# Delta-rule inverse on one orientation, with a PE turn of two heads at once and products between all four quarters of the array

## The reference

```python
a_mat = where(strict, einsum('bhnid,bhnjd->bhnij', k * beta, k) * decay, 0.0) + eye(64)
rhs = concatenate([v * beta, k * beta * exp(g)], axis=-1)
sol = triangular_solve(a_mat, rhs, left_side=True, lower=True)      # one per chunk, head and direction
u, w = sol[..., :128], sol[..., 128:]
def step(s, xs):                                                    # a scan over the chunks
    v_new = u_c - w_c @ s
    o = qd_c @ s + qk_c @ v_new
    s = s * ge_c + ke_c.T @ v_new
```

## Time and profile before

| | us |
|---|---|
| median of 3 runs | 2147.72 (2143.14 to 2150.04) |
| the profiled execution, its own time | 2146.08 |
| its span in the trace | 2144.3 |
| the stretch of the inversion, first level to the start of L2061 | 1076.9 to 1235.1 |
| PE busy over the span | 92% |
| DVE busy | 55% |
| ACT busy | 47% |

### The profile page before, as it was taken

How to read it: one execution, slowest core, us unless ns; L and a number is a source line. 1 busy time by engine, 2 the same in 40 slices (tenths; PEclk the granted TensorE clock), 3 DMA queues, 4 the chain that set the end, 5 groups by cost and what they waited for, 6 DMA issues and landing times.

```text
span 2144.3 us, 41573 instructions
## 1 busy us (share of the span) xinstructions
PE 1962.7 (92%) x16842; PEld 1729.2 (81%) x16842; DVE 1186.6 (55%) x1809; ACT 1016.2 (47%) x1592; POOL 157.3 (7%) x151
## 2 busy tenths in 40 slices
PE   6998899888899999989888889999979999898997
PEld 5783588786787787868778879999969998678997
DVE  4421578643543243354356657656767656677754
ACT  5332367523441143244633246544756655366653
POOL 0000100001000000100134410000011001011000
PEclk8999899868999999989999999999999999899999
DMA  8340268531233332333200046665545664415653
GB/s 262 97 123 29 70 206 248 160 104 42 76 98 88 89 98 88 91 90 87 70 4 4 4 117 170 186 178 149 160 116 148 185 174 146 123 45 152 186 173 113
DMA packets 441804, 254.60 MB, mean 119 GB/s; under 512 B 10817, under 2 KB 440513, under 8 KB 441537
## 3 DMA queue, kind: packets, MB, share of 16 engines
q1 hardware_dynamic: 441664, 252.59, 40.5%
HBM read 251.51 MB, written 1.05 MB: 118 GB/s over the span
## 4 chain that ended last, share of the span: by engine, by line
PE 84%; DVE 9%; ACT 3%; issue 2%; DMA 1%; POOL 0%; DVEq 0%; ACTq 0%; SPq 0%; POOLq 0%
PE bank L380 21%; PE bank L382 20%; PE bank L381 20%; PE bank L372 4%; PE bank L594 2%; PE bank L595 2%; PE bank L1958 2%; DVE weights_lo L330 2%; ACT weights_hi L323 1%; PE bank L932 1%; PE bank L1159 1%; PE bank L602 1%; PE bank L1975 1%; PE bank L1972 1%; DVE h L2578 1%
## 5 line engine op out<-in xcount | busy, mean ns | idle before, releaser
L330 DVE TENSOR_TENSOR weights_lo<-ring,weights_hi 128x1024 fp32r<-128x1024 f32 x472 | 578.0, 1228 | 363.6 <-ACT weights_hi L323 359.4
L380 PE MATMUL bank<-x_hi,weights_hi 128*128 128x256 f32 (+1 forms) x2024 | 647.2, 320 | 68.7 <-DVE x_lo L527 19.3
L323 ACT ACTIVATE weights_hi<-ring 128x1024 fp32r<-128x1024 f32 x472 | 495.4, 1054 | 389.1 <-PE bank L382 367.7
L382 PE MATMUL bank<-x_hi,weights_lo 128*128 128x256 f32 (+1 forms) x2024 | 637.7, 315 | 0.0
L381 PE MATMUL bank<-x_lo,weights_hi 128*128 128x256 f32 (+1 forms) x2024 | 637.3, 315 | 0.0
L380 PEld LDWEIGHTS bank<-x_hi,weights_hi 128*128 128x128 f32 x2024 | 389.6, 192 | 104.8 <-issue 71.0
L381 PEld LDWEIGHTS bank<-x_lo,weights_hi 128*128 128x128 f32 x2024 | 389.5, 192 | 25.8 <-issue 1.4
L382 PEld LDWEIGHTS bank<-x_hi,weights_lo 128*128 128x128 f32 x2024 | 389.0, 192 | 23.3
L380 PE MATMUL bank<-hidden_hi,weights_hi 128*128 128x256 f32 (+1 forms) x864 | 272.5, 315 | 10.0 <-DVE hidden_lo L1502 6.8
L382 PE MATMUL bank<-hidden_hi,weights_lo 128*128 128x256 f32 (+1 forms) x864 | 272.3, 315 | 0.0
L381 PE MATMUL bank<-hidden_lo,weights_hi 128*128 128x256 f32 (+1 forms) x864 | 271.6, 314 | 0.0
(11 more groups left out here) (370 smaller groups left out, 2391.4 us busy)
## 6 DMA issues: line engine op xcount, KB each, us to landing
ring<-mlp_w SPq DMA_DIRECT2D x128, 512.0 KB, 4.0
ring<-ada_w SPq DMA_DIRECT2D x96, 512.0 KB, 4.6
ring<-w_ffn_in SPq DMA_DIRECT2D x88, 512.0 KB, 4.0
ring<-w_ffn_out SPq DMA_DIRECT2D x32, 512.0 KB, 3.9
ring<-gdn_w_in SPq DMA_DIRECT2D x24, 512.0 KB, 3.9
ring<-even_w_in SPq DMA_DIRECT2D x18, 512.0 KB, 4.7
ring<-w_out SPq DMA_DIRECT2D x16, 512.0 KB, 4.0
ring<-w_in_a SPq DMA_DIRECT2D x14, 512.0 KB, 3.8
```

The source lines that it names most:

```text
L323: nc.scalar.activation(w_hi[:, g % AHEAD, :], ring[:, g % RAW, :], ACT.Copy).then_inc(hi_done[g % AHEAD].sem, 1)
L330: nc.vector.tensor_tensor(w_lo[:, g % AHEAD, :], ring[:, g % RAW, :], w_hi[:, g % AHEAD, :].bitcast(F32), ALU.subtract).then_inc(lo_done[g ...
L380: pe.matmul(dst, lhs[0](k), rhs[0](k), start=start and k == 0, stop=False)
L382: last = pe.matmul(dst, lhs[1](k), rhs[0](k), start=False, stop=stop and k == nk - 1)
```

## The change

`XX`, the second orientation, is gone. In each level PE makes the 16 products NA.XT of a unit so that even heads land on one half and odd heads on the other, and chunk 0 in one bank and chunk 1 in the other (L1963 of the changed kernel): they go between all four quarters. Then 8 transposes, each of two heads of one chunk (64 rows, 128 columns) onto all partitions (L1968), put the turned `XT` into the second half of the same two banks. ACT copies both banks to the new tile `QX` (L2152). PE makes 16 products between all quarters (L1978) and DVE copies under the mask in two halves, even and odd heads, of 128x4x64 each (L2230). `first` loses the two products that made the other orientation (L1945), ACT one copy of the unit matrix for each unit (L2134), DVE the copies of L2218 and L2226. The scaled inverses go to `XB` (a part of `QX`) and to `XW`, which all passes share.

```diff
-        DE0, NA0, XT0, XX0, QQ, GL, BB, kends = (co(2, NH, C) for _ in range(8))
+        DE0, NA0, XT0, _, QX, _, GL, BB, kends = (co(2, NH, C) for _ in range(9))
+        QX = arena[:, gdn_at + 4 * UNIT:gdn_at + 6 * UNIT].rearrange("p (z c m n) -> p z c m n", z=2, c=2, m=2)
...
         def pe_gdn_first(pe, p):
-                for c in range(2):
-                    pe.matmul(bank_of(p, z, 1)[half(1 - c), :], eye64[half(c), :], na[half(c), z].rearrange("p h c -> p (h c)"),
-                              start=True, stop=True)
...
         def pe_gdn_q(pe, p, lv):
+            xt = XT[p % 2]
             for z, u in units(p):
                 pe.wait_ge(N["xt"], nth(LEVELS + 1, p, lv, z))
-                for hd in range(NH):
+                for hp in range(4):
                     for c in range(2):
-                        ins = pe.matmul(bank_of(p, z, 0)[half(1 - c), hd * C:(hd + 1) * C], NA[p % 2][half(c), z, hd, :],
-                                        XT[p % 2][half(c), z, hd, :], start=True, stop=True)
-                ins.then_inc(N["q"], 1)
+                        for par in range(2):
+                            hd = 2 * hp + par
+                            pe.matmul(bank_of(p, z, c)[half(par), hp * C:(hp + 1) * C], NA[p % 2][half(c), z, hd, :],
+                                      xt[half(c), z, hd, :], start=True, stop=True)
+                for hp in range(4):
+                    for c in range(2):
+                        two = xt[half(c), z, 2 * hp:2 * hp + 2, :].rearrange("p h c -> p (h c)")
+                        ins = pe.transpose(bank_of(p, z, c)[:, (4 + hp) * C:(5 + hp) * C], two, eye64[half(c), :])
+                ins.then_inc(N["xr"], 1)
 
         def pe_gdn_z(pe, p, lv):
             for z, u in units(p):
-                pe.wait_ge(N["qc"], nth(LEVELS, p, lv, z))
-                pe.wait_ge(N["xx"], nth(LEVELS, p, lv, z))
-                xx = XX[p % 2]
-                for hd in range(NH):
-                    col = slice(hd * C, (hd + 1) * C)
-                    if lv < LEVELS - 1:
-                        for c in range(2):
-                            r = half(1 - c)
-                            pe.matmul(bank_of(p, z, 1)[r, col], QQ[r, z, hd, :], xx[r, z, hd, :], start=True, stop=True)
+                pe.wait_ge(N["qx"], nth(LEVELS, p, lv, z))
+                for hp in range(4):
+                    col = slice(hp * C, (hp + 1) * C)
                     for c in range(2):
-                        r = half(1 - c)
-                        ins = pe.matmul(bank_of(p, z, 0)[half(c), col], xx[r, z, hd, :], QQ[r, z, hd, :], start=True, stop=True)
+                        for par in range(2):
+                            ins = pe.matmul(bank_of(p, z, par)[half(c), col], QX[half(par), z, c, 1, col], QX[half(par), z, c, 0, col],
+                                            start=True, stop=True)
                 ins.then_inc(N["zz"], 1)
...
         def act_gdn_level(act, p, lv):
             for z, u in units(p):
-                act.wait_ge(N["q"], nth(LEVELS, p, lv, z))
-                nc.scalar.activation(QQ[:, z], compact(bank_of(p, z, 0)), ACT.Copy).then_inc(N["qc"], 1)
+                act.wait_ge(N["xr"], nth(LEVELS, p, lv, z))
+                for c in range(2):
+                    ins = nc.scalar.activation(QX[:, z, c].rearrange("p m n -> p (m n)"), bank_of(p, z, c)[:, :], ACT.Copy)
+                ins.then_inc(N["qx"], 1)
...
         def dve_gdn_level(dve, p, lv):
                 dve.wait_ge(N["zz"], nth(LEVELS, p, lv, z))
-                nc.vector.copy_predicated(xt[:, z], mask(levels[:, z, lv, :]), compact(bank_of(p, z, 0))).then_inc(N["xt"], 1)
-                if lv < LEVELS - 1:
-                    nc.vector.copy_predicated(xx[:, z], mask(levels[:, 1 - z, lv, :]), compact(bank_of(p, z, 1)))\
-                        .then_inc(N["xx"], 1)
+                m = levels[:, z, lv, :].rearrange("p (o c) -> p o c", o=1).broadcast_to((P, NH // 2, C)).bitcast(I32)
+                for par in range(2):
+                    ins = nc.vector.copy_predicated(xt[:, z].rearrange("p (h r) c -> p h r c", r=2)[:, :, par, :], m,
+                                                    four(bank_of(p, z, par)))
+                ins.then_inc(N["xt"], 1)
```

More of the change, by code:

```diff
@@ L1555, in two_block_kernel @@
         gdn_at = co.at
-        DE0, NA0, XT0, XX0, QQ, GL, BB, kends = (co(2, NH, C) for _ in range(8))
+        DE0, NA0, XT0, _, QX, _, GL, BB, kends = (co(2, NH, C) for _ in range(9))
+        QX = arena[:, gdn_at + 4 * UNIT:gdn_at + 6 * UNIT].rearrange("p (z c m n) -> p z c m n", z=2, c=2, m=2)
         def by_heads(x, c):
             return x.rearrange("p (z h c) -> p z h c", z=2, c=c)
-        DE1, NA1, XT1, XX1 = (by_heads(spare[:, i * UNIT:(i + 1) * UNIT], C) for i in range(4))
-        DE, NA, XT, XX = (DE0, DE1), (NA0, NA1), (XT0, XT1), (XX0, XX1)
+        DE1, NA1, XT1, XW = (by_heads(spare[:, i * UNIT:(i + 1) * UNIT], C) for i in range(4))
+        DE, NA, XT = (DE0, DE1), (NA0, NA1), (XT0, XT1)
+        XB = QX[:, :, 0].rearrange("p z m (h i) -> p z (m h) i", i=C)
         last_state = by_heads(arena[:, gdn_at:gdn_at + UNIT], P)
@@ L1566, in two_block_kernel @@
         last_QKT = by_heads(arena[:, gdn_at + 2 * UNIT:gdn_at + 4 * UNIT], P)
-        last_U = by_heads(arena[:, gdn_at + 5 * UNIT:gdn_at + 7 * UNIT], P)
+        last_U = by_heads(arena[:, gdn_at + 6 * UNIT:gdn_at + 8 * UNIT], P)
         qdc, SG = co(2, NH // 2, P), co(2, NH // 2, NDV)
@@ L1864, in dve_odd_in @@
             normed(VB - 1)
-        gdn_names = ("gl", "g", "d", "size", "e", "bb", "eb", "kk", "aa", "eye", "first", "q", "qc", "zz", "xt", "xx", "xb", "xw",
+        gdn_names = ("gl", "g", "d", "size", "e", "bb", "eb", "kk", "aa", "eye", "first", "xr", "qx", "zz", "xt", "xb", "xw",
                      "u", "uc", "wt", "wtc", "kend", "ws", "vn", "su", "ss", "sg", "clear", "qk", "eu", "qkt", "g2", "qe", "qd",
@@ L1943, in pe_gdn_first @@
                 na = NA[p % 2]
-                for c in range(2):
-                    pe.matmul(bank_of(p, z, 1)[half(1 - c), :], eye64[half(c), :], na[half(c), z].rearrange("p h c -> p (h c)"),
-                              start=True, stop=True)
                 for hd in range(NH):
                     for c in range(2):
-                        ins = pe.matmul(bank_of(p, z, 0)[half(c), hd * C:(hd + 1) * C], na[half(c), z, hd, :], eye64[half(c), :],
-                                        start=True, stop=True)
+                        ins = pe.matmul(bank_of(p, z, 0)[half(c), hd * C:(hd + 1) * C], na[half(c), z, hd, :], eye64[half(c), :], start=True, stop=True)
@@ L1983, in pe_gdn_values @@
                     for c in range(2):
-                        ins = pe.matmul(b[half(c), (hd % 4) * P:(hd % 4 + 1) * P], QQ[half(c), z, hd, :],
+                        ins = pe.matmul(b[half(c), (hd % 4) * P:(hd % 4 + 1) * P], XB[half(c), z, hd, :],
                                         vtok[half(c), TBS[p][z], hd * P:(hd + 1) * P], start=True, stop=True)
@@ L1994, in pe_gdn_weights @@
                         ins = pe.matmul(four(bank_of(p, z, c))[half(hd % 2), hd // 2, :],
-                                        ktk[half(c), TBS[p][z], hd * C:(hd + 1) * C], XX[p % 2][half(c), z, hd, :],
+                                        ktk[half(c), TBS[p][z], hd * C:(hd + 1) * C], XW[half(c), z, hd, :],
                                         start=True, stop=True)
@@ L2132, in act_gdn_eyes @@
                     act.wait_ge(N["xw"], u - 4 + 1)
-                nc.scalar.activation(XT[p % 2][:, z], heads(eye64), ACT.Copy)
-                nc.scalar.activation(XX[p % 2][:, z], heads(eye64), ACT.Copy).then_inc(N["eye"], 1)
+                nc.scalar.activation(XT[p % 2][:, z], heads(eye64), ACT.Copy).then_inc(N["eye"], 1)
         def act_gdn_decay(act, p):
@@ L2217, in dve_gdn_first @@
                     .then_inc(N["xt"], 1)
[L2218 removed]
         def dve_gdn_level(dve, p, lv):
[L2221 removed]
+            xt = XT[p % 2]
             for z, u in units(p):
                 dve.wait_ge(N["zz"], nth(LEVELS, p, lv, z))
[L2224 to L2228 removed]
+                m = levels[:, z, lv, :].rearrange("p (o c) -> p o c", o=1).broadcast_to((P, NH // 2, C)).bitcast(I32)
[3 more added lines that the diff above has]
+                ins.then_inc(N["xt"], 1)
+                if lv == LEVELS - 1:
                     dve.wait_ge(N["xt"], nth(LEVELS + 1, p, LEVELS, z))
[L2230 removed]
+                    nc.vector.tensor_tensor(XB[:, z], xt[:, z], per_head(beta[:, TBS[p][z], z * NH:(z + 1) * NH]), ALU.mult)\
                         .then_inc(N["xb"], 1)
```

8 lines of the change are left out of this document (2 added, 6 removed).

## The result

| | before | changed |
|---|---|---|
| median, same chip | 2146.99 us (2143.14 to 2152.77, 6 runs) | 2127.34 us (2122.25 to 2130.29, 6 runs) |
| ratio | | 0.9915 [0.9897, 0.9932] |
| span of the profiled execution | 2144.3 | 2125.5 |

The change is faster by 19.65 us, 0.9% of the time.

What follows compares the result with a forecast made beforehand. PE was taken as the bound, partly held by instructions arriving. 15.8 us less PE work, 9.0 us of new waits and 9 us fewer code stalls made -15.8, so 2132 us, range 2122 to 2142.

Steps and rivals of the forecast that it cites:

- array work: PE's first products, turns and second products in 20 levels, with `first`: 15.8 us less PE work together.
- New waits: PE waiting for ACT's two copies in seven levels, 6.3 us, and DVE's subtractions in six, 2.7: 9.0 us more.
- Code: PE's stalls for arriving instructions, 14.1 us: with 1472 fewer instructions a third is left, 9 us less.
- The counts: PE's instructions and trace: 1472 fewer instructions, some 33 packets on the instruction queue, "issue" from 14 us to about 5.
- First products and turn: Each level on PE: both units' first products 1.95 us to 1.0, with 1.12 us added for turning both.
- Rival A: The turn on PE is dear because transposes go singly: 9 us more, 2140 us; chance 0.15.
- D (two quarters): First products of even and odd heads don't overlap in four quarters: 20 us more, 2152 us; chance 0.06.
- `first`: PE's `first` without L1945: 0.3 us less than its 2.26, 1.2 us over 4.
- The sign given for it: In the changed kernel's trace, new rows of PE waiting for ACT, some 6 us.
- Rival B: PE's stalls stay, blocks being late for reasons other than density or not holding PE: 7 to 9 us more; chance 0.12.
- Rival C: PE's code is all that counts, 20 us less, waits hidden under it, or the turn is cheap: 2127 us; chance 0.12.
- rival E: PE idles in more places, so its clock drops; half the stretch's work at half clock gives 2185 us; chance 0.05.

Runs made afterwards that it cites:

- two kernels without stalls: Kernel before without L1972's products and their masked copies, 2123.63 us; changed kernel with first products of levels 1 to 4 for even heads only, 2120.01 us.
- the first experiment: Kernel before without the second orientation's products (L1972) and DVE's masked copies of them, part of the inversion left out: 2123.63 us against 2143.94.
- the turn by products: Changed kernel with each unit's turn made by 16 products with the unit matrix instead of 8 transposes, 1920 instructions more: 2146.14 us against 2143.94 before.
- the turn in four: Changed kernel with two transposes behind each pair of heads' products, eight changes of array shape a unit instead of two: 2167.73 us against 2141.64 before.
- queries later: Changed kernel with DVE's eight query-mask products of pass 2 moved behind the last masked copy of pass 3: 2126.85 us, again 2126.57.

## Why the prediction was right in its total and not in its split

The forecast was 15.8 us less, of which array work less new waits would give 6.8 and code 9. The stretch gave 16.4. The two kernels without stalls divide it: array work and waits 136.7 - 135.2 = 1.5 us, code 19.8 - 4.9 = 14.9 us. Two errors of about 5 and 6 us, of opposite sign, met: the total was right by luck. With the 0.5 us of clock and up to 1.2 us of DVE's wait set right (see the first experiment), array work and waits gave 1 to 2 us and code 14 to 15, and nothing changes in this. The step that failed is "New waits", with its "together 9.0 us", and the "Code" term of 9 us was mis-sized. (The two kernels are called "without stalls" here; 1.0 and 1.4 us of them are left.)

**The counts held**: 1472 instructions, some 33 packets (34 with the last `values`), "issue" from 14.1 us to 4.9.

**First products and turn** were right in sum: 1.02 us for a unit against 1.0 / 2 + 0.56 = 1.06. The split is 0.62 and 0.40 instead of 0.50 and 0.56: of the two changes of shape, 0.12 us fall to the products' row and 0.16 to the turn's. Rival A (transposes singly) is excluded by the 0.24 us for eight more, D (two quarters) by 0.62 against 0.91.

**`first`** became 1.87 us where 2.26 less 0.3 was expected: 0.4 less for each.

**New waits, level by level.** From the first record of a level's first products to that of the next, kernel before without stalls against changed kernel, each in a level free of stalls:

| level | without stalls | changed | gain measured | gain forecast |
|---|---|---|---|---|
| bare | 1084.40 to 1088.26, 3.86 | 1087.38 to 1091.25, 3.87 | 0.0 | 0.73 - 0.9 = -0.2 |
| with `ws` and `su`, 6 | 1114.19 to 1120.58, 6.4 | 1118.13 to 1124.69, 6.6 | -0.2 | 0.73 - 0.45 = 0.3 |
| with `keys` or the queries' products, 4 | 1120.58 to 1125.51, 4.9 | 1124.69 to 1129.39, 4.7 | 0.2 | 0.73 |
| with `weights`, 3 | 1102.24 to 1107.03, 4.8 | 1106.03 to 1110.75, 4.7 | 0.1 | 0.73 |

The bare level was forecast well: ACT's copies replace the time that the products gave up. (The sign given for it, some 6 us of PE waiting for ACT, came out at 3.1 in the rows.) The others were not. With `ws`, DVE's last subtraction ends at 1123.25 + 0.68, 3.7 us behind the start of L2036 (3.55 in the forecast), and the `su` that waits for it takes 1.0 us behind it, not 0.7: the level ends where DVE ends, and what the second products save is lost whole. With `keys` and `weights`, the forecast said that these cover the waits. They cover ACT's, but not this one: the second products of unit 1 last 0.5 us now, too short to hide the masked copy of unit 0 (0.78 us from 1128.57, or from 1109.92) for which the next level's first products wait. Before, 0.95 us of products did. The text costed that copy at its old 0.73 us "on the path", and forgot what had covered it.

Over all 20 levels, the two kernels without stalls against each other, the same records give 0.46 us for the three bare ones of pass 0 (0.53 of it in the first, where the clock was down in one of the two), -0.85 for the six with `ws`, 0.84 for the four with `keys` or the queries' products, -0.05 for the three with `weights`, and 1.07 for the four last levels with `first` and `values` behind them. That is the 1.5 us, where the forecast had -0.5, 1.7, 2.9, 2.2 and 0.5: 6.8.

**Code** was the right cause, of the wrong size. The reading of neighbouring stalls (a block in 3.35 to 3.7 us at least) gave where it hurts: dense levels stall, and fewer instructions for the same array time end it, as both kernels with products left out show.

That it is code arriving can be read from the single packets that the traces hold: in the kernel before, the changed one and the turn by products, every one of the 51 stalls (16, 11 and 24) ends 1.2 to 1.6 us behind the end of a packet of 16 KB on the instruction queue, and in these stretches no two packets start less than 3.3 us apart. A fixed time for each instruction isn't the limit: a unit's second products are 64 instructions in 0.51 us, 8 ns each, where 3.5 us for 256 would be 14. Rival B (stalls that do not come from density) is out.

But the cost was read from the idle rows, 14.1 us, and was 19 to 20 before; some 5 is left, where the forecast left 5.1. What was wrong is the sum that they were taken from. The forecast also placed what is left wrongly: it put 416 instructions of a level with `ws` in 4.5 us, but they include `su`, and such a level takes 6.6 us (4.0 for 256). Only 0.9 of the 4.9 us lie in these levels. Rival C, "code is all that counts", comes nearest to what happened: its 20 us is more than the 14 to 15 that code gave, but nearly nothing else gave anything. The Trainium skill ("Runtime: NRT & Kernel Launch", section "Instruction fetch mechanics") has this fetch mostly hidden; 19 to 20 us in the stretch before, and the 13 us or so that 1920 instructions cost in the turn by products, speak against it here.

**The clock** (rival E) stayed at 1.00 in the changed kernel's stretch through all of the new short waits. It fell only at the last `values`, in the profile of the kernel before and in one of the two of the changed kernel (the other begins its stretch with 2 us of low clock). So some 2 us of a difference between two profiled stretches can be the clock's.

What stays open: whether `su` ahead of the sums would win the DVE wait back was not tried. The 3 us by which the part behind the stretch was shorter (909.2 to 906.2 us) need no cause in the change: in the second profile of the changed kernel that part took 914.7 us.

## What to carry to other kernels

Where small fp32 products follow each other densely, count instructions beside array time: here most of the time saved came from 1472 fewer instructions, and a nearly equal turn with four-instruction products brought nothing (2146.14 us against 2143.94). A transposition on PE that avoids a second set of products pays when it is done in one group, since each change of the array's shape costs, and in four parts it cost more than the change brings (2167.73 us against 2141.64). When a run of products becomes shorter, list what it used to hide on the other engines, the copy of its neighbour unit first.

## What the runs showed of the hardware that had not been expected

- Stalls for code cost more than PE's idle rows show: 19 to 20 us for 13.1 of idle in the kernel before, and 4.9 and some 5.2 for 3.5 and 4.7 in the two profiles of the changed one. Each stall ended 1.2 to 1.6 us behind the landing of a 16 KB packet of instructions.
- A wait on a semaphore that is already satisfied is not free for PE: where 96 instructions that only wait stood between 32 products, each cost 0.06 to 0.08 us, and this `values` ran at a granted clock of 0.62.
- The clock fell at other places too in kernels that are near relatives: it was 0.50 in the first 20 us of the stretch with the turn in four, where PE was busy for 19.77 of them. At the last `values` it fell behind gaps of 2.0 us (before), 1.9 (changed), 1.5 (first products in two quarters) and 1.1 (queries later, second profile), and stayed at 1.00 behind 1.8 (before without the second orientation), 1.6 (half of the first products), 1.5 (changed, second profile) and 1.0 (queries later, first profile). What decides it was not found. Differences of 2 us and less between such kernels are the clock's as soon as theirs.
- Transposes of 64 rows onto 128 columns run in pairs from the two row halves, 0.06 us a pair, although L2077 with the same tile showed the pace of single ones. The weight loads are 134 to 142 ns here and 188 there. Source view of L1968:

```profile
L1968 PEld LDWEIGHTS bank<-tables,arena x160: 134/139/142, 1078.2 to 1167.8; 64*128 64x128 f32 x160
```
